# Differential attention in pairs of key tiles, two heads interleaved, side work in fixed slots

## What is computed

```python
# layer 0
hn = rms_norm(x, g);  z = hn @ w_in              # [Fourier 512 | q 512 | k 512 | v 512]
f = real(fft2(zf, axes=(positions, channels of each of 4 groups)))
# 4 heads, two softmax maps each (sub-queries and sub-keys of 64 channels)
p = softmax(q * 64**-0.5 @ k.T + rel_bias[t5_bucket(kpos - qpos)])
a = rms_norm((p[0] - lam * p[1]) @ v, subln_g) * (1 - lam_init)
h = x + concat(f, a) @ w_out;   h = h + swiglu(rms_norm(h))
# layer 1: GELU projection to (u, v), spatial gating in chunks of 128, projection, SwiGLU; last, RMSNorm
```

## Time and profile before

| | |
|---|---|
| time, median of 3 runs | 2104.42 us (2103.77 to 2106.22) |
| the profiled execution | 2105.68 us, its slowest core's span 2104.1 us |
| spans of the eight cores | 2088.7 to 2104.1 us |
| PE busy | 1920.1 us, 91% of the span |
| ACT busy | 941.3 us, 45% |
| DVE busy | 809.9 us, 38% |

### The profile page before, as it was taken

The page is one execution under the profiler, slowest core; times in us unless marked ns, Lnnn a source line. Parts: engine busy times, 40 slices in busy tenths (PEclk is TensorE's granted clock), DMA queues, the critical chain, the costliest instruction groups (busy, mean ns, idle before and its releaser), DMA issues.

```text
span 2104.1 us, 36130 instructions; the slowest of 8 cores (2088.7 to 2104.1 us)
## 1 busy us (share of the span) xinstructions
PE 1920.1 (91%) x12777; PEld 983.1 (47%) x12777; DVE 809.9 (38%) x1791; ACT 941.3 (45%) x1233; POOL 146.1 (7%) x169
## 2 busy tenths in 40 slices
PE   4798898888999699869999999998999999999997
PEld 3575444455555354434444444444444444444443
DVE  4682444444555454443212222213537212221146
ACT  3565777777899597623110011206565311011121
POOL 0000000000000000002210011100202221001100
PEclk7899999999999799988999999999999999999999
DMA  9221123000200700008872066441010987015612
GB/s 222 84 81 57 46 80 47 13 1 2 43 7 12 250 8 2 6 1 120 113 111 38 1 81 81 65 76 31 1 21 11 128 112 102 11 23 78 81 61 111
DMA packets 136175, 127.13 MB, mean 60 GB/s; under 512 B 9409, under 2 KB 116161, under 8 KB 136002
## 3 DMA queue, kind: packets, MB, share of 16 engines
q0 software_dynamic: 112432, 69.22, 24.6%
q1 hardware_dynamic: 23570, 55.60, 8.1%
HBM read 185.61 MB, written 8.39 MB: 92 GB/s over the span
## 4 chain that ended last, share of the span: by engine, by line
PE 81%; DVE 8%; issue 5%; DMA 3%; ACT 2%; DVEq 0%; SPq 0%; ACTq 0%
PE psum L1107 14%; PE psum L1109 14%; PE psum L1127 14%; PE psum L930 11%; PE psum L891 6%; PE psum L791 3%; PE psum L1263 3%; PE psum L1255 2%; PE psum L711 2%; PE psum L659 1%; PE psum L724 1%; PE psum L1206 1%; DVE arena L231 1%; DVE arena L326 1%; DVE arena L949 1%
## 5 line engine op out<-in xcount | busy, mean ns | idle before, releaser
L913 ACT ACTIVATE arena<-psum,arena 128x1024 bf16<-128x1024 f32 x412 | 452.5, 1117 | 112.0 <-PE psum L892 106.9
L930 PE MATMUL psum<-arena 128*128 128x129 bf16 x4096 | 331.2, 223 | 29.1 <-DVE arena L949 17.0
L1107 PE MATMUL psum<-arena 128*128 128x512 bf16 x1408 | 332.6, 379 | 1.8 <-DVE arena L231 1.8
L1109 PE MATMUL psum<-arena 128*128 128x512 bf16 x1408 | 332.6, 379 | 0.3 <-PE psum L1107 0.3
L1113 ACT ACTIVATE arena<-psum 128x512 f32<-128x512 f32 x176 | 104.9, 597 | 496.0 <-PE psum L1107 489.4
L930 PEld LDWEIGHTS psum<-arena 128*128 128x128 bf16 x4096 | 238.1, 99 | 154.0 <-issue 153.3
L1127 PE MATMUL psum<-arena 128*128 128x512 bf16 x1408 | 306.8, 379 | 0.0
L1114 DVE TENSOR_TENSOR arena<-psum,arena 128x512 bf16<-128x512 f32 x176 | 121.3, 691 | 460.6 <-PE psum L1109 454.6
L1107 PEld LDWEIGHTS psum<-arena 128*128 128x128 bf16 x1408 | 137.6, 98 | 167.2 <-issue 2.0
L1109 PEld LDWEIGHTS psum<-arena 128*128 128x128 bf16 x1408 | 137.7, 98 | 166.7 <-issue 0.8
L891 PE MATMUL psum<-arena 64*128 64x512 bf16 x512 | 200.7, 392 | 16.2 <-ACT arena L913 12.8
(11 more groups left out here) (118 smaller groups left out, 1602.3 us busy)
## 6 DMA issues: line engine op xcount, KB each, us to landing
arena<-w POOLq DMA_DIRECT2D x88, 512.0 KB, 7.0
arena<-x SPq DMA_DIRECT2D x32, 512.0 KB, 6.2
arena<-w POOLq DMA_DIRECT2D x44, 256.0 KB, 9.1
arena<-dft SPq DMA_DIRECT2D x8, 1024.0 KB, 5.8
arena<-x SPq DMA_DIRECT2D x4, 2048.0 KB, 18.6
out<-arena SPq DMA_DIRECT2D x16, 512.0 KB, 2.7
arena<-wfo SPq DMA_DIRECT2D x8, 512.0 KB, 6.7
arena<-w_uv POOLq DMA_DIRECT2D x4, 1024.0 KB, 19.6
```

What stands on the lines that cost most here:

```text
L913: k.op("act", lambda: nc.scalar.activation(out=Pb[pb], in_=Lq[i], func=AF.Exp, bias=bconst[:, col:col + 1], scale=1.0), reads=LBs + [bcons ...
L930: return lambda: nc.tensor.matmul(psum[:, c0:c0 + 129], lhsT=Pb[pb][:, idx * 128:(idx + 1) * 128], rhs=Vp[h // 2][:, kt, h % 2, 0:129], st ...
L1107: k.group("pe", [(lambda kk=kk: nc.tensor.matmul(bank(b1), lhsT=w13[sl][:, 0, kk, jj * 128:(jj + 1) * 128], rhs=hnT_[:, kk, ts], start=(kk ...
L1109: k.group("pe", [(lambda kk=kk: nc.tensor.matmul(bank(b3), lhsT=w13[sl][:, 1, kk, jj * 128:(jj + 1) * 128], rhs=hnT_[:, kk, ts], start=(kk ...
```

## The change

What it does:
1. Attention: the loop runs over 256 pairs of steps. PE's queue in a pair is `qk(G+2)`, `qk(G+3)`, `av(G)`, side work, `av(G+1)` (at an iteration's first pair the side work stands before `av(G)`). The tiles near the diagonal all take even positions. `EB` and `EBo` keep their place; head 3 gets a second table `EB2`.
2. Iterations: heads 0 and 1 as before; then (2,0) (2,1) (3,0) (3,1) (2,2) (3,2) (2,3) (3,3).
3. `pump`: one rate, 3.3 units a pair, at most 5 in a call, credit up to 12 and never below the floor; a call ends with an item. Epilogue operations: four a pair.
4. `load_outproj`: 16 loads of one residual tile, three steps apart, and the combinations of the output weights, all at fixed steps behind the load's own; the table loads follow their last use by two steps.
5. Projection: `fold_wz` runs in group 1, even/odd sums and Fourier columns one group later (group 7 does two). Group 0's weight loads wait for the second tile of x, `wzT` for the second tile of the next group, `load_x(1)` comes ahead of two constants.
6. `newton`: three operations fewer (3 + 3 x 3).

The diff, cut:

```diff
...
             for _ in range(3):
                 d(lambda: nc.vector.tensor_tensor(out=T, in0=Y, in1=Y, op=ALU.mult))
-                d(lambda: nc.vector.tensor_tensor(out=T, in0=T, in1=X, op=ALU.mult))
-                d(lambda: nc.vector.tensor_scalar(out=T, in0=T, scalar1=-0.5, scalar2=1.5, op0=ALU.mult, op1=ALU.add))
-                d(lambda: nc.vector.tensor_tensor(out=Y, in0=Y, in1=T, op=ALU.mult))
+                d(lambda: nc.vector.scalar_tensor_tensor(out=T, in0=T, scalar=-0.5, in1=X, op0=ALU.mult, op1=ALU.mult))
+                d(lambda: nc.vector.scalar_tensor_tensor(out=Y, in0=T, scalar=1.5, in1=Y, op0=ALU.add, op1=ALU.mult))
...
         k.dma("sp", gvec, gvecs_d[0:1, :].partition_broadcast(128), writes=[gvecB])
         for nm, dst, c0 in (("k", wk_s, 1024), ("v", wv_s, 1536), ("q", wq_s, 512)):
-            k.dma("pool", dst, w_in_d[:, c0:c0 + 256].rearrange("(k p) c -> p k c", p=128), writes=[wB[nm]])
-        k.dma("pool", wzT, wzT_d.rearrange("(g p) d -> p g d", p=128), writes=[wzTB])
+            k.dma("pool", dst, w_in_d[:, c0:c0 + 256].rearrange("(k p) c -> p k c", p=128), reads=[xtB[0][1]] if nm == "k" else [], writes=[wB[nm]])
+        load_x(1)
+        k.dma("pool", wzT, wzT_d.rearrange("(g p) d -> p g d", p=128), reads=[xtB[1][1]], writes=[wzTB])
...
-        load_x(1)
...
+            def fourier_cols(gz):
+                proj_z(gz, 0)
+                proj_z(gz, 1)
+                for a in pairs[gz]:
+                    if a < 8:
+                        fold2(a)
+
             n0 = 4 * (g + 1)
+            if g > 0:
+                even_odd(g - 1)
...
             do_tr(n0 + 2)
+            if g == 7:
+                fourier_cols(6)
+                even_odd(7)
...
-            if g == 0:
+            if g == 1:
                 fold_wz()
...
+            if g == 7:
+                fourier_cols(7)
+            elif g > 0:
+                fourier_cols(g - 1)
...
-        def pump(rate, flush=False):
-            fstate["credit"] = min(fstate["credit"] + rate, 4.0)
-            while fstate["credit"] >= 1.0 or flush:
-                if fstate["post"] is not None:
-                    fstate["post"]()
-                    fstate["post"] = None
+        def pump(rate, flush=False, cap=5, floor=0):
+            fstate["credit"] = max(min(fstate["credit"] + rate, 12.0), float(floor))
+            room = cap
+            while flush or (fstate["credit"] >= 1.0 and room >= 1):
...
+                u_ = it_.get("unit", 1.0)
                 i, n_ = fstate["i"], len(it_["fns"])
-                m_ = n_ - i if flush else min(n_ - i, max(1, int(fstate["credit"] / it_.get("unit", 1.0))))
+                m_ = n_ - i if flush else min(n_ - i, max(1, int(min(fstate["credit"], room) / u_)))
                 fns = [(lambda f=f: f(it_["b"])) for f in it_["fns"][i:i + m_]]
                 if not flush:
-                    fstate["credit"] -= m_ * it_.get("unit", 1.0)
+                    fstate["credit"] -= m_ * u_
+                    room -= m_ * u_
                 fstate["i"] = i + m_
                 if fstate["i"] == n_:
                     k.group("pe", fns, reads=it_["rd"], writes=[bankB[it_["b"]]], acquire=False)
                     fstate["cur"] = None
                     it_["fin"](it_["b"])
+                    if not flush:
+                        return
                 else:
                     for f in fns:
                         f()
...
-                pump(4.0)
+                pump(8.0, cap=8)
...
-                fq.append(wait_item(3))
+                fq.append(wait_item(2))
...
-            def ld_res(q4):
+            def ld_res(t):
                 xo = x.rearrange("(n p) d -> p n d", p=128)
-                bs = [hB[4 * q4 + t][hf_] for t in range(4) for hf_ in range(2)]
-                k.place(16 * q4, 16, bs)
-                k.dma("sp", hres[:, 4 * q4:4 * q4 + 4, :], xo[:, 4 * q4:4 * q4 + 4, :], writes=bs)
-
+                k.place(4 * t, 4, hB[t])
+                k.dma("sp", hres[:, t, :], xo[:, t, :], writes=hB[t])
+
+            g0 = g_now[0]
             ld(0)
-            ld(1)
-            for q4 in range(3):
-                ld_res(q4)
-            mq.extend([None] * 60)
+            at(g0 + 2, lambda: ld(1))
             for fi in range(4):
-                mq.append(lambda fi=fi: comb(fi, 0))
-                mq.append(lambda fi=fi: comb(fi, 1))
+                for half in range(2):
+                    at(g0 + 16 + 12 * fi + 4 * half, lambda fi=fi, half=half: comb(fi, half))
                 if fi < 2:
-                    mq.append(lambda fi=fi: ld(fi + 2))
-                    mq.extend([None] * 20)
-            mq.append(lambda: ld_res(3))
+                    at(g0 + 22 + 12 * fi, lambda fi=fi: ld(fi + 2))
+            for t in range(16):
+                at(g0 + (5 + 3 * t if t < 12 else 58 + 3 * (t - 12)), lambda t=t: ld_res(t))
...
-        iters = [(h_, qc_) for h_ in range(4) for qc_ in range(4)]
+        iters = [(h_, qc_) for h_ in range(2) for qc_ in range(4)] + [(2, 0), (2, 1), (3, 0), (3, 1), (2, 2), (3, 2), (2, 3), (3, 3)]
+        step_of = {it_: 32 * i for i, it_ in enumerate(iters)}
...
-        NEAR_POS = {0: [(0, 10), (1, 13), (2, 16), (3, 19), (4, 22), (16, 25)],
+        NEAR_POS = {0: [(i, 10 + 4 * i) for i in range(5)] + [(16, 30)],
                     1: [(3 + i, 4 + 4 * i) for i in range(6)],
                     2: [(7 + i, 4 + 4 * i) for i in range(6)],
-                    3: [(11 + i, 3 + 3 * i) for i in range(5)] + [(16, 18), (31, 28)]}
+                    3: [(11, 2), (12, 6), (16, 10), (13, 14), (14, 18), (31, 22), (15, 26)]}
...
+        def at(G, fn):
+            sched.setdefault(G, []).append(fn)
...
+            at(step_of[(h_, 0)] + (8 if h_ == 0 else 4), lambda h_=h_: exp_eb(h_))
+        for h_ in (1, 2):
+            at(step_of[(h_ - 1, 3)] + 27, lambda h_=h_: load_eb(h_))
+        at(step_of[(2, 1)], lambda: load_eb(3))
+        oth_uses = sorted((step_of[(h_, qc_)] + p_, h_, OTH_NEAR[(kt_, qc_)]) for h_ in range(4) for qc_ in (0, 3) for kt_, p_ in NEAR_POS[qc_] if kt_ >= 16)
+        prev_ = None
+        for G_, h_, i_ in oth_uses:
+            if prev_ is not None:
+                at(prev_ + 2, lambda h_=h_, i_=i_: load_ebo(h_, i_))
+            at(max((prev_ or 0) + 8, G_ - 8), exp_ebo)
+            prev_ = G_
...
+            ops.extend([None] * 6)
...
+        RATE = 3.3
+        NC_ = 256
+
+        def drain(n_):
+            while mq and n_ > 0:
+                op_ = mq.pop(0)
+                if op_ is not None:
+                    op_()
+                n_ -= 1
+
...
+        for c in range(NC_):
+            G = g_now[0] = 2 * c
+            for g_ in (G, G + 1):
+                for fn in sched.get(g_, ()):
                     fn()
-                softmax_tile(G)
-                if G + 2 < NG:
-                    if (G + 2) % 128 == 0 and G + 2 == 256:
-                        force_until(lambda: VB[1][15].w is not None and KTB[2][7].w is not None)
-                    if G + 2 == 384:
-                        force_until(lambda: 3 in KTB and KTB[3][7].w is not None)
-                    qk(G + 2)
-            if G >= 1:
-                av(G - 1)
-                if G % 32 == 0:
-                    while mq:
-                        op_ = mq.pop(0)
-                        if op_ is not None:
-                            op_()
-                    epi0()
-                    mq.extend([None] * 2 + epi_ops(G // 32 - 1))
-            if G < NG:
-                pump(rate_of(G))
-                for _ in range(2):
-                    if mq:
-                        op_ = mq.pop(0)
-                        if op_ is not None:
-                            op_()
-        while mq:
-            op_ = mq.pop(0)
-            if op_ is not None:
-                op_()
+                softmax_tile(g_)
+            if c + 1 < NC_:
+                if G + 2 == step_of[(2, 0)]:
+                    force_until(lambda: VB[1][15].w is not None and KTB[2][7].w is not None)
+                if G + 2 == step_of[(3, 0)]:
+                    force_until(lambda: 3 in KTB and KTB[3][7].w is not None)
+                qk(G + 2)
+                qk(G + 3)
+            first = c % 16 == 0
+            if first:
+                pump(RATE, floor=4)
+            av(G)
+            if not first:
+                pump(RATE)
+            av(G + 1)
+            if c % 16 == 15:
+                drain(1000)
+                epi0()
+                mq.extend([None] * 3 + epi_ops(c // 16))
+            drain(4)
+        drain(1000)
...
```

More of the change, by code:

```diff
@@ L532, in proj_v, with proj_z @@
                 evac(vv, bk.rearrange("p (t h e) -> p t h e", t=2, h=2), [bankB[bi]], [VB[0][2 * g + f]], eng="act")
[L534 to L536 removed]
+            def proj_z(gz, t):
+                a = pairs[gz][t]
+                rs_ = (a - 8) % 3 if a >= 8 else (2 if a == 1 and gz == 7 else 3)
                 raw_slot[a] = rs_
```

58 lines of the change are left out of this document (18 added, 40 removed).

## The result

The changed kernel takes 2084.57 us (median of four executions) against 2104.23 for the kernel before: a ratio of 0.9898, interval 0.9879 to 0.9918. One of the four executions took 2326 us with one die at a lower clock, and such executions count in no ratio of this text. The forecast was 2021 us and its range began at 1970 and ended at 2070, so the kernel got faster, as forecast, but by 20 us and not by 83. The profiled execution has a span of 2084.6 us on its slowest core, core 7, which was also the slowest in the profile of before.

What follows compares the result with a forecast made beforehand. PE's step chain with side work and waits, not ACT, was taken to bound most of attention. Attention -67, tail -7 and -0.8, first loads -4, folding -2, Newton -1.6 and -0.8 sum to -83: 2021 us, range 1970 to 2070.

Steps and rivals of the forecast that it cites:

- What stays or comes in: Attention: remaining or new waits (table exponentials, low-clock start, biased products, loads, forced side work), 45 us with side-wait and boundary charges.
- The old waits stay: Rival, attention: side-work, value-group and boundary waits remain because DVE's queue is in order; about 45 us more, 2066; chance 0.20.
- inside the 67: Attention term: 607 us of pairs plus 45 of waits, 652 against 719, -67; the removed table holes are included.
- Pairs and the new wait: Attention: PE needs 1.56 us a pair against 1.78, plus side work; odd logits waiting for ACT take back part.
- The chain formula: Attention: with two logit buffers, a pair takes 2.08 us plus 0.107 per unit of side work.
- The chain does not bind: Rival, attention: odd exponentials end before PE reaches their logits; pairs with side work cost 2.24 us, total 1980; chance 0.20.
- Side work, slots and boundaries: Attention: 707 units fit the slots; of some 46 us of side waits 7 stay; 16 iteration boundaries cost 5.
- The change doesn't do what it says: Rival, attention and tail: too few slots, side work forced in bulk, 128 output units left; 2045 us; chance 0.10.
- Tail: After attention: 64 to 72 output matmuls remain, -7 us; three fewer epilogue operations, -0.8.
- First loads and folding: Start: earlier x tiles -4 us (bounds -7, +2); fold a group later -2 (bounds -6, +3), its hole moving.
- Lower clock: Rival, attention: PE waiting at odd logits falls to its lower clock, two us more a pair; slower; chance 0.05.
- a sign of being wrong: Attention: the prediction is wrong if the clock granted from 650 to 750 us is under 0.95.

Runs made afterwards that it cites:

- a_nonear: The changed kernel with no tile treated as biased, so the 100 bias products on DVE are left out: 2017.39 us, ratio 0.9563.
- a_avlast: The changed kernel with the biased tile's value group last in its pair, behind the odd value group and side work: 2019.07 us, ratio 0.9577.
- b_spread: The kernel before with only the change's output projection loads (residual in 512 KB pieces, weight combinations at fixed steps): 2085.89 us, ratio 0.9893.
- a_bulk: The changed kernel with the residual again as three 2 MB loads at once and a fourth later: 2081.95 us, ratio 0.9893.
- a_both: The changed kernel with a_avlast's edit and epilogue operations moved behind the bias product (none in the pair ahead): 2016.21 us, ratio 0.9572.
- b_front: The kernel before with the change's first loads, fold in group 1, later Fourier columns and short Newton chains: 2097.59 us, ratio 0.9959.

## Why the prediction failed, step by step

**The failed term.** Under *What stays or comes in* the prediction charged "value groups that wait for the product of a biased tile 6 (as much as now)". That took a wait from the trace of before and kept its size, though the change rewrites the order that had made it small. In the order before, PE's queue between a tile's logits and its value group holds three steps (three value groups, the logits of the next three tiles and three slots of side work) and one logit group: 3 x 1.26 + 0.33 = 4.1 us, against the 3.16 that the tile needs by the row at 305.18. So some 0.9 us of slack covered what stood in DVE's queue. In the new order it is one pair and two logit groups: 2.43 + 0.22 + 0.31 = 2.96 us, less than the 3.16. Slack is -0.2 us before anything is queued on DVE, and a side copy (0.69) and four epilogue operations (1.6 from 723.87 to 725.46) are, right ahead of the product. These durations were all in the trace of before; the product's 1.22 us was never set against the distance. The profiles bear this out over all 100 biased tiles. From the product's end to the value group's start it takes 0.14 us at least; in the changed kernel 89 of the 100 value groups start within 0.2 us of that end, so the product is what they waited for, where in the kernel before 28 do. In `a_nonear`, where nothing waits for a product, the distance from logits to value group is 3.1 us at the median for the same tiles: the slack is none, rather than -0.2, and all that is queued on DVE comes on top. The runs put the term at 67 us (`a_nonear`), of which a new place for the value group gets 66 back (`a_avlast`) with the same work on every engine. So it is a wait and not DVE's load. The rival *The old waits stay* named DVE's queue and biased products, but priced the old waits of 45 us and not a new one.

**The holes.** The prediction put the 11.4 and 7.2 us "inside the 67" and laid their going to the pieces of the load. `b_spread` shows that they are worth 18 us in the order before; `a_bulk` shows that in the new order they go without the pieces. A forecast of this gain alone would have been near the measured time, but by luck, as the rest of the change gained and lost much more.

**Pairs and the new wait.** Right. The second logit group costs 0.22 us. The chain formula gives 2.49 us at 3.8 units and 2.08 without; measured 2.56 and 2.03. PE's waits for the exponential come to 31.8 us, none over 0.83, in about 100 pairs. The rival *The chain does not bind* is out: with the products' waits gone, pairs with side work still take 2.5 us and not 2.24 (`a_both`).

**Side work, slots and boundaries.** Right in kind, the charges too high: side matmuls wait 0.0 us in attention (7 kept) and the boundary copies hold L951 for 2.5 us (5 charged) in `a_both`, whose attention of 637.9 us is 14 less than the 652 of the sum. The slots were enough: 64 output matmuls remained, so *The change doesn't do what it says* is out. Of the waits that *The old waits stay* priced, those of side work and boundaries are gone too.

**Tail.** Right: 8.0 us measured for 7 and 0.8.

**First loads and folding.** Sized wrongly. All four tiles of x are at ACT early, the last at 13.86 us for 21.26:

```profile
8.77 1.06 ACT L288 ACTIVATE arena<-arena 128x1024 bf16<-128x1024 f32 x1 [2.49 <-DMA arena<-x]
...
13.86 1.06 ACT L288 ACTIVATE arena<-arena 128x1024 bf16<-128x1024 f32 x1
```

But the weights held back arrive late for their use (4.98 us of PE's wait), which is the late arrival that the prediction feared, for the queries and not for the keys, whose first matmul starts at 30.25 us, 7.5 earlier than before:

```profile
45.54 3.57 PE L517 MATMUL psum<-arena 128*128 128x256 bf16 x16 [4.98 <-DMA arena<-w_in]
```

and the fold's hole is 12.30 us for 12.91: it moved and did not go, as said. At the first logits 2.5 us are left of the forecast 4 + 2 + 1.6. `b_front` as a whole (8.5 us) agrees with the sum of 9.2, but most of it in the wrong place, so this agreement is luck and no proof of the steps. Behind the tail 3.3 us were gained (2.5 on the mean of the cores) for the 0.8 forecast; no run says why.

**Lower clock.** The price of a wait was underrated: the prediction had the clock fall "only behind idle of several us" and gave the case 0.05. The trace of before already spoke against that. PE waits there 1.55 us at 196.42, and from 197.05 on its matmuls take nearly double (the granted clock from 196.9 to 200.6 is 0.54):

```profile
196.42 0.38 PE L659 MATMUL psum<-arena 128*128 128x512 bf16 x1 [1.55 <-DVE arena L231]
...
197.05 1.05 PE L930 MATMUL psum<-arena 128*128 128x129 bf16 x8
```

In the changed kernel it fell behind waits of 1.2 to 2.4 us (below). From 650 to 750 us the granted clock is 0.95, at the bound that the prediction had set as a sign of being wrong; in `a_both` it is 1.00. This is part of the lost time. The granted clock in attention is 0.967 on the profiled core and 0.995 in `a_both`: of 713 and 638 us that leaves out 24 and 3, so the clock accounts for at most some 20 of the 75.5 us between the two (an estimate).

Had the products cost in the new order what they cost in the old one, the time would have been 2084.6 - 67 + 11, some 2028 us, 7 over the forecast.

## What to carry to other kernels

When a change reorders an in-order queue, don't carry a wait over from the old trace: for each consumer in the new order write down the time from its producer's start to its own place in the queue, and set it against the producer's whole path, including what stands ahead of it on every engine it passes. The one tile in five with a longer path (exponential, then a product on another engine) decides, not the usual one. If it has no slack, move its consumer behind other work that doesn't need it; here that one exchange was worth more than three times the whole change.

## What the runs showed of the hardware that was not expected

PE's clock fell behind waits of 1.2 to 2.4 us, sometimes with a delay (and three times between 190 and 250 us in the kernel before, behind waits of 1.5 to 1.6). In the changed kernel:

```profile
571.33 0.61 PE L951 MATMUL psum<-arena 128*128 128x129 bf16 x8 [2.19 <-DVE arena L938]
...
572.42 1.02 PE L951 MATMUL psum<-arena 128*128 128x129 bf16 x8
...
609.89 0.94 PE L951 MATMUL psum<-arena 128*128 128x129 bf16 x8 [1.57 <-DVE arena L299]
610.63 2.34 PE L725 MATMUL psum<-arena 128*128 128x512 bf16 x5
```

At 571.33 the eight value matmuls behind the wait still take 0.61 us, as at 2.4 GHz, and those at 572.42 take 1.02. At 610.63 five side matmuls take 2.34 us, 0.43 each after the first one's overhang, which is 512 columns at 1.2 GHz; at 2.4 they follow each other by 0.213. At 726.74 and 727.56 (above) eight value matmuls and five side matmuls take some 1.03 + 2.19 us where 0.63 + 1.24 is usual (five L673 at the full clock in this profile: 1.24), so the 2.34 us wait cost another 1.35. On this core the granted clock fell 13 times in attention after its first microseconds, each time within such a wait or at most 1.3 us behind one. But seven waits of 1.6 to 2.0 us were not followed by a fall, and no run here isolates what decides. In `a_both`, where these waits are gone, it fell once, at a wait of 1.46 us.
